# A down projection in three rounded products instead of full float32 matmuls, on weight slabs of 4 k-tiles

## What is computed

```python
u = modulate(rmsnorm(h, norm2_g), shift, scale) @ w_up        # 1024 -> 2 * 2816
a, b = split(causal_free_depthwise_conv3(u, conv_w, conv_b))
hidden = silu(a) * b                                          # 2816 wide
h = h + gate * (hidden @ w_down)                              # 2816 -> 1024
```

## Time and profile before

| | |
|---|---|
| median of 3 runs | 3085.94 us (3085.46 to 3095.84) |
| the profiled execution, own time | 3088.74 us |
| its span in the profile | 3086.9 us |
| PE busy | 2800.3 us, 91% of the span |
| DVE, ACT busy | 1747.8 us (57%), 1421.3 us (46%) |
| mean granted clock of PE | 0.942 of full |
| down projection of the first layer | 643.52 to 799.73 us, and 10.08 us more to PE's next product |

### The profile page before, as it was taken

The page is one execution under the profiler, slowest core; times in us unless marked ns, Lnnn a source line. Parts: engine busy times, 40 slices in busy tenths (PEclk is TensorE's granted clock), DMA queues, the critical chain, the costliest instruction groups (busy, mean ns, idle before and its releaser), DMA issues.

```text
span 3086.9 us, 38368 instructions
## 1 busy us (share of the span) xinstructions
PE 2800.3 (91%) x15278; PEld 2262.3 (73%) x15278; DVE 1747.8 (57%) x1811; ACT 1421.3 (46%) x1575; POOL 29.6 (1%) x40
## 2 busy tenths in 40 slices
PE   6999889999897998857689999899999999999998
PEld 4875368854685898747469997677877878778786
DVE  3224355520444685352335544487888888887886
ACT  3235133310234454310134443376767677676675
POOL 0001000000001000000000000000000000000000
PEclk8999999999998999977689999999999999999999
DMA  7547222222231344300014443188989889898986
GB/s 298 194 165 270 82 82 102 81 75 77 96 143 60 139 164 176 115 1 1 1 55 164 167 175 111 51 322 317 367 326 359 323 322 369 322 364 307 343 329 230
DMA packets 84932, 589.78 MB, mean 191 GB/s; under 512 B 9936, under 2 KB 10064, under 8 KB 21328
## 3 DMA queue, kind: packets, MB, share of 16 engines
q1 hardware_dynamic: 83376, 576.16, 50.4%
q10 hardware_dynamic: 1440, 11.93, 1.0%
HBM read 587.01 MB, written 1.05 MB: 191 GB/s over the span
## 4 chain that ended last, share of the span: by engine, by line
PE 81%; DVE 9%; ACT 5%; DMA 3%; issue 2%; DVEq 0%; SPq 0%; POOL 0%; ACTq 0%; POOLq 0%
PE banks L449 23%; PE banks L443 19%; PE banks L444 19%; PE banks L445 18%; DMA ring<-in_stream 3%; DVE ring_rounded L505 1%; ACT aT_rounded L2542 1%; ACT ring_rounded L495 1%; PE banks L2450 1%; DVE rstd L696 1%; DVE activations L1256 0%; PE banks L772 0%; ACT scratch L836 0%; DVE nmax L808 0%; DVE scratch_rounded L2629 0%
## 5 line engine op out<-in xcount | busy, mean ns | idle before, releaser
L444 PE MATMUL banks<-ring_rounded,activations_rounded 128*128 128x512 f32 x1344 | 530.8, 395 | 0.0
L505 DVE TENSOR_TENSOR ring_rounded<-ring,ring_rounded 128x2048 fp32r<-128x2048 f32 (+3 forms) x150 | 302.7, 2021 | 395.8 <-ACT ring_rounded L495 395.0
L444 PE MATMUL banks<-aT_rounded,ring_rounded 128*128 128x256 f32 (+1 forms) x1552 | 501.3, 323 | 0.0
L495 ACT ACTIVATE ring_rounded<-ring 128x2048 fp32r<-128x2048 f32 (+3 forms) x150 | 253.6, 1695 | 325.4 <-PE banks L445 310.2
L444 PEld LDWEIGHTS banks<-aT_rounded,ring_rounded 128*128 128x128 f32 x1552 | 301.9, 195 | 20.9
L443 PE MATMUL banks<-aT_rounded,ring_rounded 128*128 128x256 f32 x960 | 276.3, 288 | 21.1 <-DVE aT_rounded L718 11.6
L444 PEld LDWEIGHTS banks<-ring_rounded,activations_rounded 128*128 128x128 f32 x1344 | 254.7, 189 | 53.0
L2623 DVE TENSOR_TENSOR ring_rounded<-ring,tables_rounded 128x2048 fp32r<-128x2048 f32 x112 | 253.6, 2286 | 43.1 <-ACT tables_rounded L2542 42.7
L445 PE MATMUL banks<-aT_rounded,ring_rounded 128*128 128x256 f32 x960 | 274.8, 286 | 0.0
L2542 ACT ACTIVATE tables_rounded<-ring 128x2048 fp32r<-128x2048 f32 x112 | 215.0, 1920 | 123.3 <-DMA ring<-in_stream 105.5
L2623 DVE TENSOR_TENSOR ring_rounded<-ring,aT_rounded 128x2048 fp32r<-128x2048 f32 x112 | 254.3, 2286 | 22.9 <-ACT aT_rounded L2542 22.4
(11 more groups left out here) (297 smaller groups left out, 5096.7 us busy)
## 6 DMA issues: line engine op xcount, KB each, us to landing
ring<-in_stream SPq DMA_DIRECT2D x491, 1024.0 KB, 5.4
ring<-in_stream SPq DMA_DIRECT2D x48, 704.0 KB, 5.4
ring<-in_stream SPq DMA_DIRECT2D x28, 768.0 KB, 5.9
activations<-in_rpb ACTq DMA_DIRECT2D x2, 1536.0 KB, 6.4
tables<-in_tab_b ACTq DMA_DIRECT2D x1, 2436.0 KB, 8.3
tables<-in_tab_a ACTq DMA_DIRECT2D x1, 2304.0 KB, 8.6
hT<-in_h ACTq DMA_DIRECT2D x1, 2048.0 KB, 15.6
ring<-in_stream SPq DMA_DIRECT2D x4, 512.0 KB, 6.2
```

The lines of the kernel that those rows point to most:

```text
L444: pe.matmul(out, exact(upper), exact(w_lower), start=False, stop=False)
L495: act.activation(exact(upper), w, ACT.Copy).then_inc(g.s["act_pieces"], 1)
L505: dve.tensor_tensor(exact(w), w, rounded(upper), ALU.subtract).then_inc(g.s["dve_pieces"], 1)
```

## The change

The down projection of the first layer (l = 0) becomes a split stage. Its slabs are cut by rows: one slab of 2 k-tiles and five of 4 (`DOWN_ROWS`), each with all 1024 outputs. PE goes through the k-tiles in order and at each through all eight outputs with three rounded products, so that eight PSUM banks are open at once (outputs 2 and 3 in banks 6 and 7, the others in the short ones). In the last half slab the order turns round: output by output, two k-tiles each, and the sum of squares for output m - 2 behind output m, the last two behind all. The mean square of the next norm uses a short bank now.

The hidden tiles are split into upper and lower too. The upper parts have twelve places: the four tiles of `g.sq` (tiles 0 to 3, split during the up projection), and the eight of `g.aT`, each used in turn (tiles 4 to 21, split once the up projection is over; tiles 12 to 21 once the tile that held the place is multiplied).

```diff
+DOWN_ROWS = [(0, 2)] + [(a, 4) for a in range(2, KF, 4)]
...
-        cols("w_down", l, [r(P * i, P) for i in range(KD)], KF)
+        if l == 0:
+            for a, kt in DOWN_ROWS:
+                out.append(("down_rows", l, kt, [(a, D)]))
+        else:
+            cols("w_down", l, [r(P * i, P) for i in range(KD)], KF)
...
-        kind = g.long_kind(0 if key == ("n1", 0) else 1)
+        kind = "six" if key == ("n1", 0) else "short" if key == ("n1", 1) else "long"
...
+        half = kt // 2
+        for h in range(2):
+            pe.wait_ge(g.s["dve_pieces"], g.at("piece", g.piece_of[n] + h))
+            if h and a + kt == KF:
+                break
+            for kk in range(half * h, half * h + half):
+                pe.wait_ge(g.s["dve_feedforward"], g.at("hidden", l, a + kk))
+                for m in range(KD):
+                    if a + kk == 0:
+                        kind = "long" if m in (2, 3) else "short"
+                        pe.wait_ge(*g.bank_free(kind))
+                        banks[m] = g.open(("dn", l, m), kind)
+                    last = one(m, kk)
+            last.then_inc(g.s["pe_pieces"], 1)
+            g.count("pe_pieces", ("piece used", g.piece_of[n] + h))
+        g.also("pe_pieces", ("used", n))
...
     for m in range(KD):
-            last = mm(pe, ps[:, 0:T], w[:, P * k:P * k + P], g.hid[:, k, 0:T], k == 0, k == KF - 1)
-        last.then_inc(g.s["pe_feedforward"], 1)
-        if m:
-            sum_pe(g, pe, norm, T, m - 1)
-    sum_pe(g, pe, norm, T, KD - 1)
+        for kk in range(half, kt):
+            last = one(m, kk)
+        last.then_inc(g.s["pe_feedforward"], 1)
+        g.count("pe_feedforward", ("mm", "dn", l, m))
+        if m >= 2:
+            sum_pe(g, pe, norm, T, m - 2)
+    g.also("pe_feedforward", ("used", n))
+    g.also("pe_feedforward", ("piece used", g.piece_of[n] + 1))
+    for k in range(KD - 2, KD):
+        sum_pe(g, pe, norm, T, k)
...
+def hidden_slots(p):
+    return [p] if p < 2 else [2 * p - 2, 2 * p - 1]
...
+            upper = g.hid_upper(t)
+            if 4 <= t < 12:
+                act.wait_ge(g.s["pe_feedforward"], g.at("mm", "up", l, KF - 1, 1))
+            elif t >= 12:
+                act.wait_ge(g.s["pe_pieces"], g.at("piece used", g.down_piece + 1 + (t - 8) // 2))
...
+    for p in range(2, KF // 2 + 1):
+        for k in hidden_slots(p):
+            if k >= 4:
+                upper_hidden(k)
+        upper_act(g, act, 1)
...
+        g.hid_upper = lambda k: g.sq[:, k, :] if k < 4 else g.aT[:, (k - 4) % KD, :]
```

More of the change, by code:

```diff
@@ L253, in lay_out @@
             lo[:, 2560:3584] = x["mla_wukv_0_2"]
+            continue
+        if name == "down_rows":
+            a = lists[0][0]
+            w = x["w_down"][layer, P * a:P * (a + kt)]
+            stream[n, :, :kt * D] = w.reshape(kt, P, D).transpose(1, 0, 2).reshape(P, -1)
             continue
@@ L1357, in ffn1_pe @@
         return
-    for m in range(KD):
[L1359 to L1366, removed]
-            last = mm(pe, ps[:, 0:T], w[:, P * k:P * k + P], g.hid[:, k, 0:T], k == 0, k == KF - 1)
+    banks = {}
@@ new lines, in ffn1_pe, with one @@
+    for a, kt in DOWN_ROWS:
+        n, _ = g.next_weights()
+        pieces = [piece(g, g.piece_of[n] + h) for h in range(2)]
+        def one(m, kk):
+            wl, wu = pieces[kk // (kt // 2)]
+            c = slice(D * (kk % (kt // 2)) + P * m, D * (kk % (kt // 2)) + P * m + P)
+            k = a + kk
+            return mm3(pe, banks[m][:, 0:T], wu[:, c], wl[:, c], g.hid_upper(k), g.hid[:, k, 0:T], k == 0, k == KF - 1)
+        half = kt // 2
[14 more added lines that the diff above has]
+        g.also("pe_pieces", ("used", n))
@@ L1368, in ffn1_pe @@
+    for k in range(KF - half, KF):
+        pe.wait_ge(g.s["dve_feedforward"], g.at("hidden", l, k))
+    for m in range(KD):
+        for kk in range(half, kt):
+            last = one(m, kk)
         last.then_inc(g.s["pe_feedforward"], 1)
         g.count("pe_feedforward", ("mm", "dn", l, m))
-        g.also("pe_feedforward", ("used", n))
-        if m:
-            sum_pe(g, pe, norm, T, m - 1)
-    sum_pe(g, pe, norm, T, KD - 1)
+        if m >= 2:
+            sum_pe(g, pe, norm, T, m - 2)
@@ L1384, in upper_hidden @@
         g.count("act_feedforward", ("upper hidden", l, t))
     for t in range(KF + 1):
-        if t < KF and t % 2 == 0 and (l == 1 or t // 2 < last):
+        if t < KF and t % 2 == 0:
             upper_act(g, act, 1)
@@ L1402, in ffn1_act @@
             g.count("act_feedforward", ("silu", l, t - 1))
-        if l == 1 and t >= 2:
+        if t >= 2 and (l == 1 or t < 6):
             upper_hidden(t - 2)
-        if t < KF and t % 2 == 1 and (l == 1 or t // 2 < last):
+        if t < KF and t % 2 == 1:
             upper_act(g, act, 1)
@@ L1444, in ffn1_dve @@
             g.count("dve_feedforward", ("hidden f32", l, t - 1))
-            if l == 0:
-                g.also("dve_feedforward", ("hidden", l, t - 1))
-        if l == 1 and t >= 2:
+        if t >= 2 and (l == 1 or t < 6):
             lower_hidden(t - 2)
-        if t < KF and t % 2 == 1 and (l == 1 or t // 2 < last):
+        if t < KF and t % 2 == 1:
             lower_dve(g, dve, 1)
@@ L1452, in ffn1_dve @@
         lower_hidden(KF - 1)
+        return
+    for p in range(2, KF // 2 + 1):
+        for k in hidden_slots(p):
+            if k >= 4:
+                lower_hidden(k)
+        lower_dve(g, dve, 1)
 SHIFTED = 14
@@ L3018, in build @@
         g.n2_upper = n2_upper
+        g.hid_upper = lambda k: g.sq[:, k, :] if k < 4 else g.aT[:, (k - 4) % KD, :]
+        g.down_piece = g.piece_of[next(n for n, x in enumerate(g.slabs) if x[0] == "down_rows")]
         second_places(g)
```

16 lines of the change are left out of this document (9 added, 7 removed).

## The result

The changed kernel takes 3059.55 us (median of 4 runs, 3056.89 to 3067.36), the kernel before 3087.95 us in the same comparison. The ratio is 0.9905, with a 95% interval of 0.9882 to 0.9929. Forecast were 3059 us and a shortening of 0.9%.

The account below looks back on a forecast made before the run. PE's instruction stream was taken to bound the kernel. Stage -32.2, tail +4.3 and clock +0.9 make -27.0 us, so from a median of 3085.94 the forecast was 3059 us, range 3054 to 3066.

Parts of the forecast that it names:

- The two prices: PE in the down projection: 0.858 us for a plain float32 matmul, 0.2267 us for a rounded product.
- The rule of four passes: Skill page's count for a true FP32 matmul: 0.907 us each, the stage 41 us shorter; the measured row was preferred.
- No waits at the start: Start of the down projection: PE never waits, with 0.9 us to spare at piece 1 and 1.0 at piece 2.
- No waits later: Later pieces of the down projection: PE does not wait, since some 6.5 us stay at each hand-over.
- The tail gives 4.3 us back: Behind output 7: two next-slab pieces on ACT and DVE delay the last sum to 6.1 us, from 1.8.
- The clock: 0.9 us for the last sum: Last sum behind output 7: after idling, PE runs it at 1.2 GHz, which adds 0.9 us.
- Late pieces: Rival: PE waits at hand-overs of down-projection pieces; 5 to 12 us come back, 3064 to 3071 us; chance 0.10.
- A free tail: Rival: ACT and DVE reach the two pieces early enough, so the tail costs nothing; 3054 us; chance 0.05.
- The low clock in the bank rotation: Rival: PE falls to 1.2 GHz turning through eight banks in the down projection; 105 us more, 3164 us; chance 0.02.
- Something moved in the rest: Rival: the second layer goes out of step with loads or banks, taking back over 12 us; 3071 to 3085; chance 0.03.
- The sum of -27.0: Whole kernel: -32.2 us for the down projection, +4.3 for the tail, +0.9 for the clock.
- The stage (-32.1 for -32.2): Down projection up to the end of output 7: 124.0 us instead of 156.2, 32.2 us less if PE never waits.

Follow-up runs that it names:

- e3: The changed kernel with its new slabs, order and eight open banks, but plain float32 matmuls and nothing split in the down projection; 3092.26 us, ratio 1.0004.
- e4: The changed kernel with the upper part of each piece of the down projection made three times on ACT; one run, 3058.12 us.
- e1: The changed kernel with two pieces of the second layer's first slab moved, one ahead of the third add and square, one into the next norm; 3058.81 us.
- e6: As e1, but the first piece's upper part on ACT ahead of the fourth square, its lower on DVE ahead of the fifth add; 3055.38 us, ratio 0.9904.
- e5: The changed kernel with the two loops inside a piece turned, so PE stays in one PSUM bank for six products instead of three; one run, 3066.69 us.
- after_again: The changed kernel run again without an edit; 3059.69 us, ratio 0.9904.
- after_third: The changed kernel run once more, side by side with a repeat of e6; 3058.56 us, ratio 0.991.

## Why the prediction was right

Point by point, in its own order:

- **The two prices.** 0.858 us a plain matmul and 0.2267 a rounded product: e3 has 155.35 us for 181 of the one kind (0.858), and the changed kernel 124.09 for 528 products and five sums, with 124.0 forecast. Shown. The rule of four passes in the Trainium skill ("FP8 and Floating Point Precision", section "TensorE Precision Notes"), with a rounded product as the price of a pass, gives by an estimate 9 us more of gain. The chip gives 3.8 rounded products for one plain matmul. That does not refute four passes: a quarter of 0.858 us is 0.2145 us, and the estimate took 0.2267 for it. Why a rounded product is 0.012 us dearer than that quarter no run shows.
- **No waits at the start.** Margins of 0.9 and 1.0 us were worked out, 0.96 and 0.95 measured. e4 shows that no other hand-over is as tight, and that piece 1 has 0.8 us more on ACT than I worked out, since I took ACT and DVE as one chain.
- **No waits later.** 6.5 us of margin: with 3.8 us more on each hand-over PE waited at none of the nine.
- **The tail gives 4.3 us back.** It gives 4.0. e1 and e6 show that the two pieces are the cause, and that all of it can be had again. The mechanism was right in each place: ACT's and DVE's pairs took 2.84 and 3.43 us, as in the earlier trace rows.
- **The clock: 0.9 us for the last sum.** This term was wrong in the changed kernel's profile and right as a possibility. The sum took 1.13 us there and 2.07 in e4, behind equal idle time. A case like that of the earlier trace rows showed that it can happen, not that it does; it should have gone into the range, not into the sum.
- **The rivals.** Late pieces: not seen. In e4 3.0 us of late pieces took 4.8, since the clock fell behind the second of them; I had priced the wait alone. A free tail: refuted for the order as written, though an order that has it can be written (e6). The low clock in the bank rotation: e5 and the clock of 1.00 in the stage refute it here. So this case does not agree with what the Trainium skill ("TensorE: Matmul & The Clock Gate", section "A second HAM failure mode: psum-queue depth-cycling") tells of another kernel: PE turned through eight banks, was never idle and kept its clock. Something moved in the rest: up to the experts the difference is 1592.1 - 1564.9 = 27.2 us (means over two and three profiles), and stage and gap alone are 28.1. So about 1 us is lost on the way, nearly all of it behind the first norm of the second layer (1184.8 us from there to the experts' norm before, 1185.6 now). The sum had this at nothing, with up to 3 us in its bounds; its cause is open.

So the mechanism was right, and the closeness of the total is in part luck. The sum of -27.0 meets the 27.2 measured up to the experts because two misses offset each other: 0.9 us for the clock that were not spent, and about 1 us in the second layer that was not counted. The stage (-32.1 for -32.2) and the tail (4.0 for 4.3) need no luck. The 28.4 us between the medians hold the experts' scatter besides. And the forecast started from 3085.94 us, the median of before at the time; from the 3087.95 us of the comparison it would have been 3061. That 3059 and 3059.55 are half a microsecond apart is luck within a scatter of several.

## What to carry to other kernels

When a stage that was slow for each output gets a faster inner loop or finishes its outputs all at the end, look for what other engines did in the gaps between its outputs: here two weight pieces cost nothing while outputs came 19.7 us apart, and 4 us when they came 2.2 apart. An earlier place in the same queues made them free again (e6). Price a kind of instruction by the distance of its starts in a dense stretch of the same form; that gave the stage to 0.1 us. And before believing a difference between two spans, find the places in both traces where a norm puts all engines in step, and compare stretch by stretch: the whole of the changed kernel scattered by 12 us over its runs, the stretch up to the experts by 0.6 over its three profiles.

## What the runs showed that I had not expected

The experts' stage took from 1079.3 to 1088.3 us over twelve profiles of kernels that do not differ in it, while up to that stage equal kernels agree to 0.6 us. PE's idle time behind output 7 was 3.95 us in all five profiles with that tail, and the last sum took 1.13, 1.20, 1.13, 2.07 and 1.12 us (the changed kernel, after_again, after_third, e4, e5): the same idle time does not give the same clock. In e4 the clock also fell behind 2.18 us of idle PE, which cost 1.8 us more; that is one case.
